# A two-layer gated scan on one core: when the next head's preparation is issued, and what the first layer's scan issues first

## The reference

```python
def _chunk_gated_scan(q, k, v, log_g):
    b = jnp.cumsum(log_g, axis=2)                       # inside a chunk of 32 tokens
    ref = b[:, :, CHUNK // 2 - 1:CHUNK // 2]
    s = jnp.einsum('bnthk,bnshk->bnhts', q * jnp.exp(b - ref), k * jnp.exp(ref - b))
    s = jnp.where(np.tril(np.ones((CHUNK, CHUNK), bool)), s, 0.0)
    o_intra = jnp.einsum('bnhts,bnshv->bnthv', s, v)
    b_last = b[:, :, -1]
    q_dec = q * jnp.exp(b)
    k_dec = k * jnp.exp(b_last[:, :, None] - b)
    def step(state, xs):
        qd, kd, vc, bl = xs
        o = jnp.einsum('bthk,bhkv->bthv', qd, state)
        state = jnp.exp(bl)[..., None] * state + jnp.einsum('bthk,bthv->bhkv', kd, vc)
        return state, o
    ...
def bidirectional_gated_scan(q, k_fwd, g_fwd, k_bwd, g_bwd, v):
    fwd = _chunk_gated_scan(q, k_fwd, v, g_fwd)
    bwd = flip(_chunk_gated_scan(flip(q), flip(k_bwd), flip(v), flip(g_bwd)))
    ...
# second layer: 12 heads; q, both gates, v and the output gate are slices of h @ w_in
# g = log(f), k = 1 - f, f = lb + (1 - lb) * sigmoid(z)
```

## Time and profile before

| | |
|---|---|
| median of 3 runs | 4059.78 us (4050.93 to 4068.09) |
| the profiled execution, its own time | 4055.85 us |
| its span (first to last instruction) | 4054.2 us |
| mean granted clock of TensorE | 0.927 of full |
| TensorE busy, VectorE, POOL, ACT | 88%, 45%, 29%, 27% of the span |
| first layer's scan begins | at 689 us of the span |
| second layer's scan, step 0 to its end | 1371 to 2215 us |

### The profile page before, as it was taken

The page is one execution under the profiler, slowest core; times in us unless marked ns, Lnnn a source line. Parts: engine busy times, 40 slices in busy tenths (PEclk is TensorE's granted clock), DMA queues, the critical chain, the costliest instruction groups (busy, mean ns, idle before and its releaser), DMA issues. The chain is left out here.

```text
span 4054.2 us, 47003 instructions
## 1 busy us (share of the span) xinstructions
PE 3560.9 (88%) x16369; PEld 2321.4 (57%) x16369; DVE 1821.6 (45%) x4038; ACT 1081.7 (27%) x2206; POOL 1179.5 (29%) x948
## 2 busy tenths in 40 slices
PE   8989998999798999999987698998877776949996
PEld 4645676777344667567546347564556775524442
DVE  1025552443573456666665460323479476240011
ACT  1023333442342233332432450221213212101111
POOL 0000000343343455555564362001212444211110
PEclk9999998999899999999999896998987877969998
DMA  3264542231532111211212532123334722347996
GB/s 116 68 183 143 151 133 86 80 103 58 217 147 60 55 57 45 66 56 41 72 38 71 220 137 76 47 64 101 105 86 144 252 75 101 121 185 241 319 320 233
DMA packets 409824, 494.01 MB, mean 122 GB/s; under 512 B 70514, under 2 KB 314506, under 8 KB 409603
## 3 DMA queue, kind: packets, MB, share of 16 engines
q1 hardware_dynamic: 380983, 457.42, 34.0%
q0 software_dynamic: 4608, 16.78, 1.6%
q10 hardware_dynamic: 24012, 16.97, 1.3%
HBM read 362.32 MB, written 128.77 MB: 121 GB/s over the span
## 5 line engine op out<-in xcount | busy, mean ns | idle before, releaser
L821 POOL TENSOR_TENSOR hgrn_queries<-hgrn_qd,hgrn_pair_decay 128x640 f32<-128x640 f32 x192 | 279.4, 1475 | 290.5 <-PE hgrn_ps_a L936 255.6
L871 PE MATMUL hgrn_ps_w<-xT,hgrn_ring 128*128 128x512 f32 x432 | 195.8, 600 | 1.8 <-PEq L34 1.8
L395 PE MATMUL gla_bg_ps<-gla_bg_w,xT 128*128 128x256 f32 x768 | 186.6, 388 | 4.3 <-DMA gla_bg_w<-in_w_in_ab_dram 4.3
L1473 PE MATMUL end_ps_z<-end_w,end_yT 128*128 128x512 f32 x384 | 168.7, 600 | 1.8 <-DMA end_w<-in_w_out_ab_dram 1.1
L2577 PE MATMUL end_ps_z<-end_w,end_yT 128*128 128x512 f32 x384 | 168.4, 599 | 0.8 <-ACT end_yT L2505 0.8
L395 PEld LDWEIGHTS gla_bg_ps<-gla_bg_w,xT 128*128 128x128 f32 x768 | 145.1, 194 | 35.0 <-issue 10.6
L391 PE MATMUL att_bg_ps<-xT,att_bg_w 128*128 128x512 f32 (+1 forms) x288 | 136.6, 614 | 13.3 <-POOL att_ident L1780 13.3
L45 POOL MEMSET gla_ident<- 128x128 f32 x1 | 0.2, 204 | 483.3 <-POOLq L34 483.3
L871 PEld LDWEIGHTS hgrn_ps_w<-xT,hgrn_ring 128*128 128x128 f32 x432 | 81.7, 193 | 94.1 <-issue 93.9
L871 PE MATMUL hgrn_ps_w<-hgrn_xs,hgrn_wsum 128*128 128x512 f32 x288 | 129.8, 599 | 5.3 <-ACT hgrn_sig L1153 5.3
L1041 DVE TENSOR_TENSOR hgrn_k_end<-hgrn_kd,hgrn_end_decay 128x128 f32<-128x128 f32 x168 | 127.1, 796 | 9.2 <-issue 2.6
(11 more groups left out here) (645 smaller groups left out, 7744.2 us busy)
## 6 DMA issues: line engine op xcount, KB each, us to landing
expw_wg<-in_exp_w_gate_dram SPq DMA_DIRECT2D x16, 2048.0 KB, 10.3
expw_wu<-in_exp_w_up_dram SPq DMA_DIRECT2D x16, 2048.0 KB, 16.3
expw_wd<-in_exp_w_down_dram SPq DMA_DIRECT2D x16, 2048.0 KB, 21.9
att_w_ada<-in_ada_w_dram SPq DMA_DIRECT2D x24, 1024.0 KB, 6.3
hgrn_ring<-in_w_in_c_dram SPq DMA_DIRECT2D x18, 1024.0 KB, 5.4
end_gt<-gate_l SPq DMA_DIRECT2D x16, 768.0 KB, 8.5
hgrn_ring<-in_w_in_c_dram SPq DMA_DIRECT2D x24, 512.0 KB, 5.5
hgrn_o<-hgrn_o_stage SPq DMA_DIRECT2D x192, 64.0 KB, 1.6
```

Of the source, the lines that this page charges most:

```text
L395: last = pe.matmul(bank[0:job.rows, q * job.width:(q + 1) * job.width], job.acts[:, k, t * P:t * P + job.rows], w[:, k, 0:job.width], star ...
L821: pool.tensor_tensor(queries[:, d, s, :].rearrange("p (b a c) -> p b a c", b=POINTS, a=PC), q, f, ALU.mult).then_inc(queries_done, 1)
L871: last = pe.matmul(bank[:, :], a[:, k, :], x(k), start=(fresh and k == 0), stop=(k == HK - 1), skip_group_check=True)
L1473: made = pe.matmul(ps_z[h][:, :], yT[:, k, :], w[:, k, h * BANK:(h + 1) * BANK], start=(k == 0), stop=(k == NB - 1))
```

## The change

In `projected_scan` the second half of a head's preparation is issued later. On VectorE `sums(1)` goes from p = 3 to p = 4, `spans_of(1)` from p = 4 to p = 5, beside `grown(0)`, which stays there; `grown(1)` stays at p = 6. On ACT `exps(1)` goes from p = 4 to p = 5, and `decays` from p = 5 to p = 6. On POOL the two `scale_keys_in` go from p = 5 and 6 to p = 6 and 7. In `low_rank_scan` the wait for the constants and the two transposes go behind the first gate products and background matmuls, right ahead of `front(0)`. No instruction is added, removed or changed in size.

```diff
@@ projected_scan, POOL
                 scale_queries(h, p)
-                if h + 1 < heads and p in (5, 6):
-                    scale_keys_in(h + 1, p - 5)
+                if h + 1 < heads and p in (6, 7):
+                    scale_keys_in(h + 1, p - 6)
@@ projected_scan, VectorE
                     sums(h, 0)
                 elif p == 3:
                     spans_of(h, 0)
+                elif p == 4:
                     sums(h, 1)
-                elif p == 4:
+                elif p == 5:
                     spans_of(h, 1)
-                elif p in (5, 6):
-                    grown(h, p - 5)
+                    grown(h, 0)
+                elif p == 6:
+                    grown(h, 1)
@@ projected_scan, ACT
-                elif p in (3, 4):
-                    exps(h, p - 3)
-                elif p == 5:
+                elif p in (3, 5):
+                    exps(h, p // 2 - 1)
+                elif p == 6:
                     decays(h, 0)
                     decays(h, 1)
@@ low_rank_scan, TensorE
-            pe.wait_ge(consts, 1)
-            for d in range(2):
-                pe.transpose(ps_s[:, d * P:(d + 1) * P], ident[:, :], ident[:, :])
             pe.wait_ge(low_loaded, 96)
             for d in range(2):
                 for half in range(2):
@@
                 bg.multiply(pe, 2 * d + 1)
             bg.multiply(pe, LEAD)
+            pe.wait_ge(consts, 1)
+            for d in range(2):
+                pe.transpose(ps_s[:, d * P:(d + 1) * P], ident[:, :], ident[:, :])
             front(0)
```

## The result

| | before | after |
|---|---|---|
| median | 4059.78 us (4050.93 to 4068.09, 5 runs) | 4034.02 us (4029.42 to 4035.82, 5 runs) |
| ratio to before, 95% interval | | 0.9938 (0.9926 to 0.9950) |
| profiled execution, its own time | 4055.85 us | 4034.02 us |
| span, granted clock | 4054.2 us, 0.927 | 4032.3 us, 0.931 |

The forecast was 4035 us. The two profiled spans differ by 21.9 us and the two medians by 25.8, where the sum had 25.

A forecast was written before the change was run, and what follows sets the result against it. TensorE was taken as the bound, so only its waits counted: 20.0 us in odd heads, 2 in head 8 and 3 in head 10, 25 us in sum, gave 4035 us beside the median; range 4017 to 4058 us.

The forecast's parts named there:

- Term 3: Head 8: the first scores of head 9 come 2 us earlier, VectorE's own work being the bound; bounds 0 and 11.2 us.
- Term 4: Head 10: as in head 8, but p = 4 has a fill for TensorE; 3 us gained, bounds 0 and 6.0 us.
- term 1: Odd heads: `sums(1)` a step later ends five join waits, 13.2 us, and four clock falls, 6.8 us; 20.0 us gained.
- Rival B: Odd heads: the wait moves on one step, to p = 4, giving back term 1's 20 us; 4055 us, chance 0.15.
- rival C: Head ends, p = 6 and 7: the next head's first queries are late, slower, 4089 us at 6 us lateness; chance 0.05.
- Term 2: Even heads 0, 2, 4, 6: no wait of this kind and nothing for VectorE to join at p = 4; 0 us.
- Rival A: Heads 8 and 10 give nothing, as VectorE is busy in 92% of these stretches; sum 20.0 us, 4040 us, chance 0.15.
- The rule on the port: VectorE and POOL share a port pair; moving L806 only shifts its cost, so heads 8 and 10 gain nothing: 20 us, not 25.
- Terms 5 and 6: ACT's `exps(1)` and decays one step later, and POOL's 22 moved L806: 0 us each.
- Term 7: First layer: gate products wait for the DMA of gla_shift anyway; 0 us, bounds 10.6 us gained and 0.7 lost.

The follow-up runs named there:

- joins ahead of `sums(1)`: Kernel before with one edit: in odd heads at p = 3 VectorE does its joins between `spans_of(0)` and `sums(1)`; 4038.72 us, ratio 0.9953.
- late order in odd heads alone: Kernel before with the whole VectorE, ACT and POOL move only while heads 1, 3, 5, 7 and 9 run; 4040.98 us, ratio 0.9947.
- the scan moved ahead: Changed kernel, old order in heads 0, 2, 4, 6, and L992 of `sums(1)` at p = 3 while heads 8 and 10 run; 4029.65 us, ratio 0.9934.

## Why the prediction was right, point by point

**The sum was nearer than its terms.** The forecast of 4035 us lies 1 us from the measured median, and that is luck. The profiled pair differs by 21.9 us, and the light heads, terms 3 and 4, gave 1.0 us with the steps behind them where the sum had 5. What carries the change is term 1.

**Term 1, odd heads: right, 20.0 forecast and 21.3 measured.** The steps are 9.00 us, not 9.25, since TensorE pays a little more than its wait: 11.89 us with a wait of 2.64 against 9.00 without. The joins' place is the cause (joins ahead of `sums(1)`, late order in odd heads alone), the clock's part is in the 45.0 us at a granted clock of 1.00, and the spare of 5 us is 5.5. Rival B was far off, and so was rival C: the six waits for POOL's queries all lie in the stretch from head 8 on, none at the first tile of heads 1 to 7.

**Term 2, even heads: wrong by 1.5 us.** The step said "at p = 4 nothing for VectorE to join" and did not look at p = 5, to which `spans_of(1)` moved, beside `grown(0)` and ahead of two joins of a three-fill step. The order on VectorE alone does not make the joins late, though: with POOL's products at their old places the same order gave 49.97 us. It is L806 beside L1021, 2.3 us for 0.33, that does, so the 1.5 us come from the two moves together, each of which the sum had at 0.

**Term 3, head 8: right as far as it went.** I had the scores 6.0, 15.7 and 25.1 us behind those at 2021.05; they came 5.8, 15.7 and 24.5 us behind those at 2006.41. **Term 4, head 10: 1.4 instead of 3 us.** What both leave out is the step behind. The old last waits of 0.44 us became 3.41 and 3.29 us, and the granted clock of what follows fell from 1.00 to 0.75 and from 0.99 to 0.70: 1.5 us in head 8 and, over two steps, 1.5 in head 10. I had priced the falls of the clock that go with old waits and none that come with new ones. So the light heads give 4.0 and take back 3.0. That the new wait brings the fall holds well behind head 10: in the five traces with a wait of 2.9 to 3.7 us there the next step is 5.05 to 5.71 us long, in the eight others 4.37. Behind head 8 it is open: the step took 5.12 us behind a wait of 3.40 in one kernel and 6.80 behind one of 1.89 in another. Rival A, "the light heads give nothing", is nearly right in its size: forecast 20, measured 21.9 in all.

**The rule on the port.** Rows: L992 took 4.44 us beside L806 and 2.28 alone, and with L806 cut short the heads named there lost 13 us. The Trainium skill's rule ("SBUF — State Buffer", "Who interferes with whom"), that the second of two instructions stands still, agrees, and so does its other half, that a VectorE instruction with at most one input in SBUF is safe, unless it runs in one of the two-port modes, which a copy can enter. Of two instructions by tile (duration in ns, min/median/max) the one with an operand in PSUM keeps its time over the whole scan, and the copy does not (in which mode it ran, no run shows):

```profile
L1071 DVE SCALAR_TENSOR_TENSOR hgrn_state<-hgrn_state,hgrn_end_decay,hgrn_ps_s x144: 339/344/350, 1385.6 to 2192.6; 128x128 f32<-128x128 f32 x144
L999 DVE COPY hgrn_mids<-hgrn_cum x24: 188/2110/2127, 1284.4 to 2134.7; 128x32 f32<-128x32 f32 x24
```

As a forecast the rule would have given 20 us, mine 25, and the 21.9 lie nearer to it.

**Terms 5 and 6: the zero was right for ACT, and for POOL in sum only.** With ACT and POOL left behind 32 us of waits for ACT appear. With POOL alone left behind the scan is 6.5 us longer, since odd heads lose 3.6 us and heads 8 and 10 4.3, while even heads win 2.4; the rest is 1.7 us in head 9's step p = 1, less 0.7 in the lead of the scan. So POOL's move costs the even heads their time, and the other heads need it; the prediction spoke of the moves as if they could only cost.

**Term 7, first layer: right.** The DMA was the wait, 10.51 us.

Outside these terms, 0.8 us are the lead of the scan, which takes 129.9 us in eight of the thirteen profiled executions here and 130.5 to 130.7 in five, with no tie to the edits; 1.9 us are outside the scan: 0.4 in the first layer's start, the rest in stages in which nothing changed.

## What to carry to other kernels

Where a fill waits for a short join, ask what long work the joining engine has in front of it, and put the join first; one reordered line gave most of this gain. When a producer moves a step, move its consumers on every in-order engine with it: an engine at 27% busy can still hold the whole kernel, because what counts is what queues behind its wait. But look at what the moved instruction then runs beside: POOL's product at its new place made a VectorE instruction of 0.33 us take 2.3. Price the clock on both sides: a wait that goes can give its fall back, and one of some 3 us that comes in its place can bring a new one.

## What the runs showed that I had not expected

- POOL pays the port as VectorE does: a product of 32 columns took 0.25 us at least, 1.21 us in the median and 2.18 at most. So a small instruction is no small one there, and moving a 2.35 us product from POOL to VectorE, where it takes 1.22 us, made two heads, in which VectorE is the busy engine, 4.2 us shorter in one trace, 1.5 of them by the clock of one step.
- The fall of the clock behind a wait of 2.6 to 2.7 us is no fixed price: of the five such waits at p = 4 before, four brought it and one did not, and the same wait of 2.67 us ahead of head 9's step p = 1 brought it in six of the eleven experiments (10.3 to 11.9 us for the step) and in neither of the traces before and after (9.00 us). A gain of under 2 us in one profiled execution can be this alone, as in head 8 with the scan moved ahead.
